# An mLSTM layer on one core: per-chunk rows spread over the partitions by DMA instead of TensorE, and each chunk's heads handled in two halves

## The chip, the cores and the metric

One NeuronCore of a Trainium2 chip runs the whole program. The metric is the device time of one execution in microseconds. Engines are TensorE (PE), VectorE (DVE), ScalarE (ACT), GpSimd (POOL) and SyncE (SP, here only a DMA queue); each executes its own instruction list in order and they meet through semaphores.

## The reference, cut to what matters

With DEPTH = 1 the reference is one layer: an mLSTM mixer and a SwiGLU feed-forward, each behind an RMS norm and with a residual. Sizes: 2048 tokens, width 1024, 8 heads with 64 query/key and 128 value columns, feed-forward width 2816, all float32.

```
u = rmsnorm(x);  q, k, v, o_pre, if_pre = split(u @ w_in)
cum_f = cumsum(log_sigmoid(f));  log_d[t, s] = cum_f[t] - cum_f[s] + i[s]   (s <= t, else -inf)
m_t = max(cum_f + m_state, max_s log_d);  w_inter = exp(cum_f + m_state - m_t)
scores = (q k^T) * exp(log_d - m_t)
num = w_inter * (q C) + scores v;  den = w_inter * (q n) + sum(scores)
h = num / max(|den|, exp(-m_t));  C, n, m carried to the next chunk
x = x + (rms(h) * g * sigmoid(o_pre)) @ w_out;  x = x + swiglu(rmsnorm(x))
```

## The kernel before, in words

The 2048 tokens are worked in two halves of 1024 (`h`). Each half goes through the same stages in turn: norm and transposes of the input (a prologue), the input projection (84 units of 12 matmuls of 128x512, `project`), a chunk loop over 8 chunks of 128 tokens, the second norm, and the feed-forward (`feed_group`, `drain`). Every float32 product is made as three matmuls of a high and a low part (`three_passes`, `project`); the high part is a cast on ACT, the low part a subtraction on DVE. All orders are written out by hand, engine by engine.

The change is in the chunk loop and what feeds it. Gate values (forget sums, their running maximum, the input gate) are computed as rows: tiles `t0` to `t4` of 8 heads x 512 tokens, by `gate_part` on DVE and ACT, spread over the units of the projection by the list `GATE_DVE`. A chunk needs two of these rows on all partitions: minus the running maximum (for the decay matrix) and `w_inter` (for the queries, and its last column for the decay of the state). The kernel before does this on TensorE. `gate_part` stores the rows as high and low parts in `negm` and `wint`, and for each chunk:

- `spread(c)` writes a mask of -1e30 above the diagonal into two PSUM banks by two bf16 matmuls of 128x512 (line 2055) and adds the row of each head by eight matmuls of 128x128 with a selecting matrix `pick` (line 2058). ACT's `decay_matrix` then takes the exponential of each head out of PSUM, with a bias per partition (line 1028).
- `weights(c)` spreads `w_inter` by four matmuls (line 2084), and transposes the keys (line 2090). DVE's `weigh_queries` copies the last column (`dec`, line 1566) and multiplies the queries (line 1569).

The rest of a chunk: `scores` (line 2072), `weigh_keys` (line 1575) and `weigh_scores` (line 1584) on DVE, `state_sums` (line 2139) and `outputs` (lines 2153, 2157) on TensorE. Then DVE's `update_state` (line 1603), ACT's copies into `num` (lines 1085, 1088) and squares, DVE's `head_scale_a` and `head_scale_b`, which end in `hrow` (line 1642). TensorE transposes the eight heads (`turn_heads`, line 2164), DVE gates them (`gate_heads`, line 1591), ACT and DVE split the result (`hg_high`, line 1102; `hg_low`, line 1596), and `out_tile` multiplies with `w_out` (lines 1884 to 1886). DVE adds the product to the residual (`add_out`, line 1651) and in the first chunks prepares `w_out` (`split_out`, line 1528).

TensorE's order in the loop for chunk `c` is: spread, scores, weights(c), the first half of out_tile(c-3, 1), turn_heads(c-1), its second half, state_sums(c), outputs(c), turn_v(c+1), out_tile(c-1, 0). DVE's order is: weigh_queries, weigh_keys, weigh_scores(c), gate_heads(c-1), add_out(c-3, 1), hg_low(c-1), update_state(c), head_scale(c), norm2_rows(c-3), add_out(c-1, 0), and in chunks 1 and 2 a run of split_out. SP issues the loads of a chunk (`load_qkc`, `load_vtc`, `load_og`, 512 KB each) in a fixed order, each behind waits for the buffer it fills. POOL stores the projection and loads the residual tiles (`load_res`, 1 MB each).

Of the kernel before, what the change touches and what calls it, by code (L numbers as in the profile page):

```python
# [5 lines left out]
F32 = mybir.dt.float32  # L6
# [6 lines left out]
P = 128  # L13
# [44 lines left out]
GATE_DVE = (0, 0, 8, 9, 10, 11, 12, 13, 14, 18)  # L58
# [66 lines left out]
def mlstm_layer(nc, x, mix_norm_g, ffn_norm_g, w_gate, w_up, w_down, w_in, b_if, norm_g, w_out, out):  # L125
# [8 lines left out]
    with ExitStack() as ctx:  # L134
# [49 lines left out]
        negm = place("negm", r_a, [P, TOK], F32R)  # L184
        wint = place("wint", r_a + 4 * KB, [P, TOK], F32R)
# [8 lines left out]
        v1 = [place(f"v1_{s}", r_q + 16 * KB + s * HEADS * VW * 4, [P, HEADS, VW], F32) for s in range(2)]  # L194
        dmat = place("dmat", r_c + 12 * KB, [P, HEADS, P], F32)
# [36 lines left out]
        ident_b = small("ident_b", [P, P], BF16)  # L232
        pick = small("pick", [P, HEADS, P], F32R)
        mask = small("mask", [P, 4, P], BF16)
# [7 lines left out]
        dec = small("dec", [P, 4])  # L242
# [6 lines left out]
        pick_src = place("pick_src", r_q, [P, HEADS, P], F32)  # L249
# [10 lines left out]
        h_hbm = nc.dram_tensor("h_hbm", [SEQ // P, P, D], F32, kind="Internal").ap()  # L260
        proj_hbm = nc.dram_tensor("proj_hbm", [HALVES, 3, TILES, P, 8, P], F32, kind="Internal").ap()
# [4 lines left out]
        EPS_SET, IDENT_SET, PICK_SET, CONST_SET = 1, 3, 6, 12  # L266
# [5 lines left out]
        raw_loaded = [sem(f"raw_loaded{s}") for s in range(2)]  # L272
        qkc_loaded = [sem(f"qkc_loaded{s}") for s in range(2)]
# [15 lines left out]
        const_dve = sem("const_dve")  # L289
# [37 lines left out]
        wint_spread = sem("wint_spread")  # L327
# [3 lines left out]
        dec_done = sem("dec_done")  # L331
# [138 lines left out]
        def spread_bank(c):  # L470

            return 0 if c < 2 else 4

# [20 lines left out]
        def _(sp):  # L494
# [25 lines left out]
            for h in range(HALVES):  # L520
                if h == 0:
# [45 lines left out]

                sp.wait_ge(p_lo_done, h * PU + unit_at(10, 6) + 1)
# [16 lines left out]
                load_qkc(2)  # L585
                load_og(1)
# [74 lines left out]
        def _(pool):  # L661
# [6 lines left out]
            nc.gpsimd.memset(pick_src[:, :, :], 0.0).then_inc(const_pool, 1)  # L668
            for row in (0, 32):
                pool.wait_ge(const_pool, 4 + (1 if row else 0))  # L670
                nc.gpsimd.affine_select(out=pick_src[:, :, :], in_=pick_src[:, :, :], compare_op=ALU.not_equal,
                                        fill=1.0, base=-row, pattern=[[-1, HEADS], [0, P]], channel_multiplier=1)\
                    .then_inc(const_pool, 1)
            nc.gpsimd.memset(mask[:, :, :], 0.0).then_inc(const_pool, 1)
# [3 lines left out]
            pool.wait_ge(const_pool, 10)  # L678

            nc.gpsimd.affine_select(out=mask[:, :, :], in_=mask[:, :, :], compare_op=ALU.is_ge, fill=MASKED, base=0,  # L680
                                    pattern=[[0, 4], [1, P]], channel_multiplier=-1).then_inc(const_pool, 1)
# [19 lines left out]
            for h in range(HALVES):  # L701
# [22 lines left out]
                for tile in (cols[:, :], negm[:, :].bitcast(F32), wint[:, :].bitcast(F32)):  # L724
                    nc.gpsimd.memset(tile, 0.0).then_inc(prep_done, 1)

                def store_block(g, k):
# [6 lines left out]
                        .then_inc(p_last_stored if (g, k) == (PG - 1, 1) else p_stored[g % 2], 16)  # L734

# [89 lines left out]
        def _(act):  # L825
# [42 lines left out]
            for h in range(HALVES):  # L868
# [99 lines left out]
                if h == 0:  # L968
                    proj_hi(h, 4)
# [1371 lines left out]
```

## Time and profile before

| | us |
|---|---|
| time, median of 3 runs (lowest, highest) | 2154.73 (2153.97, 2157.39) |
| the profiled execution's own time | 2154.42 |
| its span in the trace | 2152.8 |
| TensorE busy in the span | 2121.9 |
| VectorE busy | 1425.7 |
| ScalarE busy | 939.2 |
| GpSimd busy | 250.1 |

The span is from the first to the last instruction in the trace; the execution's own time has 1.6 us around it. Busy is the time in which an engine had at least one instruction under way. Matmuls overlap in the trace (a 128x512 matmul shows 0.39 us, and one starts every 0.23 us), so what a matmul takes from its successors is read from the distance of starts. The granted clock of TensorE was full over nearly all of the span.

### The profile page before, as it was taken

Reading aid. Unit: us, or ns where it says so; the run is one execution under the profiler, and the core shown is the slowest. Engines: PE = TensorE matmul, PEld = TensorE weight load, DVE = VectorE, ACT = ScalarE, POOL = GpSimd, SP = SyncE. Lnnn points to the kernel's source line nnn. Section 1 sums busy time; section 2 is a strip of 40 time slices with the busy share of each in tenths; the row PEclk is TensorE's granted clock in tenths of the full one; section 3 lists DMA queues with packets and bytes.
Section 4 is the critical chain, followed back from the end, with each engine's and each line's share of the span. In section 5 each row is a group of like instructions: output and inputs, shape, how many; then the busy total and the mean of one; then the engine's idle time right before and its main releaser. Section 6 shows DMA issues by size and latency. Waiting matters only on the chain.

```text
span 2152.8 us, 29471 instructions
## 1 busy us (share of the span) xinstructions
PE 2121.9 (99%) x10424; PEld 1762.6 (82%) x10440; DVE 1425.7 (66%) x2274; ACT 939.2 (44%) x1686; POOL 250.1 (12%) x357
## 2 busy tenths in 40 slices
PE   6999999999999999999999999999999999999999
PEld 5888888888888888888878888888888888888887
DVE  8765476787566565679677644767866657556764
ACT  5433674453333333345444347544533333334443
POOL 3211100021001010100121111001110101001000
PEclk9999999999999999999999999999999999999999
DMA  4333373223322334773414334632233232357443
GB/s 148 110 110 113 109 272 121 84 69 106 105 96 97 117 102 150 270 249 118 152 64 142 118 94 147 233 119 89 68 103 109 97 117 96 105 190 250 152 134 107
DMA packets 200288, 281.56 MB, mean 131 GB/s; under 512 B 12912, under 2 KB 131696, under 8 KB 200176
## 3 DMA queue, kind: packets, MB, share of 16 engines
q1 hardware_dynamic: 171696, 183.07, 26.5%
q0 software_dynamic: 28480, 97.02, 12.9%
q8 instruction: 68, 1.11, 0.2%
q14 instruction: 44, 0.36, 0.1%
HBM read 197.73 MB, written 82.31 MB: 130 GB/s over the span
## 4 chain that ended last, share of the span: by engine, by line
PE 94%; DVE 3%; DMA 1%; ACT 1%; issue 1%; POOL 0%; SPq 0%; DVEq 0%; POOLq 0%
PE ps L2247 13%; PE ps L2250 13%; PE ps L2249 13%; PE ps L1971 7%; PE ps L1975 7%; PE ps L1973 7%; PE ps L2295 6%; PE ps L2297 6%; PE ps L2299 6%; PE ps L1884 3%; PE ps L1886 3%; PE ps L1885 3%; PE ps L1891 2%; PE ps L2157 1%; DMA res<-in_x_dram 1%
## 5 line engine op out<-in xcount | busy, mean ns | idle before, releaser
L1722 DVE TENSOR_TENSOR ring<-raw_f,ring 128x512 fp32r<-128x512 f32 x308 | 211.4, 687 | 188.1 <-ACT ring L1148 186.6
L1148 ACT CAST ring<-raw_f 128x512 fp32r<-128x512 f32 x308 | 191.2, 623 | 208.7 <-PE ps L2250 193.2
L2247 PE MATMUL ps<-u_lo,ring 128*128 128x512 f32 x704 | 275.7, 392 | 0.0
L2250 PE MATMUL ps<-u_hi,ring 128*128 128x512 f32 x704 | 274.1, 389 | 0.0
L2249 PE MATMUL ps<-u_hi,ring 128*128 128x512 f32 x704 | 273.9, 389 | 0.0
L2295 PE MATMUL ps<-ring,ring 128*128 128x512 f32 x616 | 240.5, 390 | 2.0 <-DVE ring L1801 1.9
L2299 PE MATMUL ps<-ring,ring 128*128 128x512 f32 x616 | 239.7, 389 | 0.0
L2297 PE MATMUL ps<-ring,ring 128*128 128x512 f32 x616 | 239.7, 389 | 0.0
L2247 PE MATMUL ps<-t_op,ring 128*128 128x512 f32 x528 | 206.0, 390 | 0.0
L2250 PE MATMUL ps<-t_op,ring 128*128 128x512 f32 x528 | 205.5, 389 | 0.0
L2249 PE MATMUL ps<-t_op,ring 128*128 128x512 f32 x528 | 205.4, 389 | 0.0
L1190 ACT CAST ring<-g_in 128x512 fp32r<-128x512 f32 x154 | 95.6, 621 | 217.4 <-PE ps L2299 215.8
L1795 DVE TENSOR_TENSOR ring<-g_in,ring 128x512 fp32r<-128x512 f32 x154 | 106.3, 690 | 106.0 <-ACT ring L1190 106.0
L795 POOL DMA_DIRECT2D ops_hbm<-kept x154 | 83.6, 543 | 759.1 <-DVE kept L1820 559.6
L1321 DVE TENSOR_TENSOR pring<-raw,pring 128x512 fp32r<-128x512 f32 x132 | 90.7, 691 | 109.7 <-ACT pring L864 108.9
L1815 DVE TENSOR_TENSOR kept<-ps,kept 128x512 f32<-128x512 f32 x132 | 90.9, 689 | 105.7 <-PE ps L2250 105.7
L2250 PEld LDWEIGHTS ps<-u_hi,ring 128*128 128x128 f32 x704 | 132.1, 188 | 27.6
L2247 PEld LDWEIGHTS ps<-u_lo,ring 128*128 128x128 f32 x704 | 132.2, 188 | 27.1 <-issue 0.5
L2249 PEld LDWEIGHTS ps<-u_hi,ring 128*128 128x128 f32 x704 | 132.2, 188 | 26.9
L1971 PE MATMUL ps<-u_lo,pring 128*128 128x512 f32 x384 | 151.7, 395 | 2.4 <-DVE u_lo L1309 2.4
L1975 PE MATMUL ps<-u_hi,pring 128*128 128x512 f32 x384 | 150.3, 391 | 0.0
L1973 PE MATMUL ps<-u_hi,pring 128*128 128x512 f32 x384 | 150.3, 391 | 0.0
(223 smaller groups left out, 4180.3 us busy)
## 6 DMA issues: line engine op xcount, KB each, us to landing
ops_hbm<-kept POOLq DMA_DIRECT2D x154, 256.0 KB, 2.4
g_in<-ops_hbm SPq DMA_DIRECT2D x154, 256.0 KB, 2.7
raw<-in_ml_w_in_dram SPq DMA_DIRECT2D x24, 1024.0 KB, 5.4
proj_hbm<-pkept POOLq DMA_DIRECT2D x96, 256.0 KB, 2.7
raw_f<-in_ffn_w_gate_dram SPq DMA_DIRECT2D x44, 512.0 KB, 4.7
raw_f<-in_ffn_w_up_dram SPq DMA_DIRECT2D x44, 512.0 KB, 4.6
b<-in_ffn_w_down_dram SPq DMA_DIRECT2D x88, 256.0 KB, 4.6
x_in<-in_x_dram SPq DMA_DIRECT2D x16, 512.0 KB, 6.3
```

The lines of the kernel that those rows point to most:

```text
L1148: nc.scalar.copy(four(ring[slot][:, 0, :]), feed_source(q, s)).then_inc(w_hi_done, 1)
L1722: nc.vector.tensor_tensor(four(ring[slot][:, 1, :]), feed_source(q, s), four(ring[slot][:, 0, :].bitcast(F32)), ALU.subtract).then_inc(w_l ...
L1795: nc.vector.tensor_tensor(ring[e % 3][:, 1, :], g_in[e % 4][:, :], ring[e % 3][:, 0, :].bitcast(F32), ALU.subtract).then_inc(ea_lo_done, 1)
L1971: pe.matmul(banks(bank), w[:, 0, now], moved(kind, 1, k), start=(fresh and k == 0), stop=False, skip_group_check=True)
L1973: pe.matmul(banks(bank), w[:, 0, now], moved(kind, 0, k), start=False, stop=False, skip_group_check=True)
L1975: last = pe.matmul(banks(bank), w[:, 1, now], moved(kind, 0, k), start=False, stop=(k == 3), skip_group_check=True)
L2247: pe.matmul(banks(bank), wh, moved(kind, 1, k), start=(fresh and k == 0), stop=False, skip_group_check=True)
L2249: pe.matmul(banks(bank), wh, moved(kind, 0, k), start=False, stop=False, skip_group_check=True)
L2250: last = pe.matmul(banks(bank), wl, moved(kind, 0, k), start=False, stop=(k == 3), skip_group_check=True)
L2295: pe.matmul(banks(bank + j), a[:, 0, now], w[:, 1, :], start=(fresh and n == 0), stop=False, skip_group_check=True)
L2297: pe.matmul(banks(bank + j), a[:, 0, now], w[:, 0, :], start=False, stop=False, skip_group_check=True)
L2299: last = pe.matmul(banks(bank + j), a[:, 1, now], w[:, 0, :], start=False, stop=(n == GROUPS - 1), skip_group_check=True)
```

## The change

The rows go out to a DRAM tensor and come back spread over the partitions.

- `negm`, `wint`, `pick`, `ident_b`, `dec`, TensorE's `spread` and the first half of `weights` go (what is left is `turn_keys`), and so do step 9 of `gate_part` and two ACT copies per call of it.
- POOL's `store_rows` writes `t4` and `t2` of each half of the gate rows to `rows_hbm`, after projection groups 1 and 4. SP's `load_rows(c)` reads them back: one DMA for `negb` (8 heads x 128 tokens, the same for 128 partitions, 512 KB) and two for `wq` (one head of each pair for each half of the partitions, 256 KB together). It stands ahead of the first load of `w_out` for chunks 0 and 1, and right behind `load_qkc(c)` from chunk 2 on, with waits for the slot's readers.
- DVE's `mask_rows(c)` adds the mask to `negb` in place. It stands within the last projection group for chunks 0 and 1, and between hg_low(c-1) and update_state(c) for chunk c+1.
- `weigh_queries` and `update_state` read `wq`; `decay_matrix` reads `negb`, from SBUF.
- `hrow` is made, transposed and gated in two halves of four heads. `h_done` and `h_turned` now count halves.
- `load_res(0)` moves ahead of the last projection store. A few steps of the prologue, of the second norm and of the passage to the second half change places. TensorE's unit 83 is now cut in two equal parts around `turn_keys(1)` and `turn_v(1)`.

```diff
+                def store_rows(t):
+                    for kind, tile in ((0, t4), (1, t2)):
...
+                        pool.dma_start(rows_hbm[h, kind, 4 * t:4 * t + 4, :].rearrange("c (p n) -> p c n", n=P),
+                                       tile[:, :].rearrange("p (c n) -> p c n", n=P)).then_inc(rows_stored, 16)
+                def load_rows(c):
+                    s = c % 2
+                    if c >= 2:
+                        sp.wait_ge(dmat_done, h * 64 + 8 * (c - 1))
+                        sp.wait_ge(qw_done, h * 8 + c - 1)
+                        sp.wait_ge(state_done, h * 32 + 4 * (c - 1))
+                    sp.dma_start(negb[s][:, :, :].rearrange("p i t -> p (i t)"),
+                                 rows_hbm[h, 0, c:c + 1, :].partition_broadcast(P)).then_inc(negb_loaded[s], 16)
+                    for a in range(2):
+                        rows = rows_hbm[h, 1, c, :].rearrange("(g a n) -> a g n", a=2, n=P)
+                        sp.dma_start(wq[s][64 * a:64 * a + 64, :, :], rows[a].partition_broadcast(64))\
+                            .then_inc(wq_loaded[s], 16)
                 load_qkc(2)
+                load_rows(2)
                 load_og(1)
...
                 for c in range(3, TILES):
                     load_qkc(c)
+                    load_rows(c)
                     load_vtc(c)
+                def mask_rows(c):
+                    dve.wait_ge(negb_loaded[c % 2], h * 64 + 16 * (c // 2) + 16)
+                    nc.vector.tensor_tensor(negb[c % 2][:, :, :], negb[c % 2][:, :, :],
+                                            mask[:, :].unsqueeze(1).broadcast_to([P, HEADS, P]), ALU.add)\
+                        .then_inc(darg_done, 1)
                     if c:
                         hg_low(c - 1)
+                        if c + 1 < TILES:
+                            mask_rows(c + 1)
                     update_state(c)
-                def spread(c):
-                    for half in range(2):
-                        pe.matmul(banks(spread_bank(c) + half), ident_b[:, :], mask[...], start=True, stop=False)
-                        for i in range(4):
-                            last = pe.matmul(ps[...], pick[:, 4 * half + i, :], negm[:, now], stop=(i == 3))
-                    for g in range(4):
-                        last = pe.matmul(ps[:, 2, g * P:g * P + P], pair, wint[:, tile_cols(c)], ...)
 def gate_heads(c):
+                    for half in range(2):
+                        some = slice(4 * half, 4 * half + 4)
+                        dve.wait_ge(h_turned, h * 16 + 2 * c + half + 1)
+                        last = nc.vector.tensor_tensor(og[c % 2][:, some, :], ..., og[c % 2][:, some, :], ALU.mult)
 def turn_heads(c):
+                    for half in range(2):
+                        pe.wait_ge(h_done, h * 16 + 2 * c + half + 1)
+                        for i in range(4 * half, 4 * half + 4):
+                            last = pe.transpose(ps[:, 4 + half, ...], hrow[:, i, :], ident[:, :])
+                        last.then_inc(h_turned, 1)
 the second norm
-                feed_low(0, 3)
                 op_lo(st + 1, 5)
+                feed_low(0, 3)
```

## Rows read from the trace of the kernel before

**Rows 1.** The page, parts 1 and 4: busy time; the chain that ended last, by engine.
```profile
PE 2121.9 (99%) x10424; PEld 1762.6 (82%) x10440; DVE 1425.7 (66%) x2274; ACT 939.2 (44%) x1686; POOL 250.1 (12%) x357
...
PE 94%; DVE 3%; DMA 1%; ACT 1%; issue 1%; POOL 0%; SPq 0%; DVEq 0%; POOLq 0%
```
**Rows 2.** TensorE's instructions by line: busy us, mean ns, idle before.
```profile
L2058 PE MATMUL ps<-negm,pick 128*128 128x128 f32 x128 | 22.0, 309 | 0.0
L2084 PE MATMUL ps<-wint,pick 128*128 128x128 f32 x64 | 10.3, 283 | 0.0
L2055 PE MATMUL ps<-mask,ident_b 128*128 128x512 bf16 x16 | 6.2, 390 | 0.0
```
**Rows 3.** Windows (us of the span): busy PE, PEld, DVE, ACT, POOL; clock, DMA share, GB/s.
```profile
264.00:330.00 66.00, 63.91 (x470) 54.12 (x472) 46.17 (x91) 42.38 (x86) 6.18 (x11) 1.00 0.65 239
330.00:411.00 81.00, 81.00 (x581) 68.90 (x584) 52.48 (x112) 33.77 (x76) 2.92 (x5) 1.00 0.35 118
```
**Rows 4.** Timeline, a steady chunk: start, duration, engine, line, what [idle before].
```profile
340.45 0.10 PEld L2055 LDWEIGHTS ps<-mask,ident_b 128*128 128x128 bf16 x1 [0.26 <-issue]
...
341.80 1.16 PE L2072 MATMUL ps<-qkc 64*128 64x128 f32 x16
...
342.89 0.66 PE L2084 MATMUL ps<-wint,pick 128*128 128x128 f32 x4
...
343.39 0.63 PE L2090 MATMUL ps<-ident,qkc 128*128 128x128 f32 x4
...
344.40 0.68 DVE L1575 TENSOR_TENSOR kw<-ps,colt 128x512 f32<-128x512 f32 x1
...
350.34 1.10 PE L2139 MATMUL ps<-v,kw 128*64 128x129 f32 x16
...
351.12 1.22 DVE L1596 TENSOR_TENSOR hg_lo<-og,hg_hi 128x1024 fp32r<-128x1024 f32 x1
...
354.56 1.13 DVE L1603 SCALAR_TENSOR_TENSOR state<-state,dec,ps 128x129 f32<-128x129 f32 x4 [2.21 <-PE ps L2157]
```
**Rows 5.** Timeline, chunk 0 into chunk 1 of the first half.
```profile
283.20 1.41 DVE L1528 SCALAR_TENSOR_TENSOR wo<-wo_raw,head_g,wo 128x512 fp32r<-128x512 f32 x2 [1.61 <-ACT wo L1010]
...
284.59 1.13 DVE L1603 SCALAR_TENSOR_TENSOR state<-state,dec,ps 128x129 f32<-128x129 f32 x4
...
292.43 1.06 PE L2164 MATMUL ps<-ident,hrow 128*128 128x128 f32 x8 [0.99 <-DVE pkept L1456]
```
**Rows 6.** Timeline, chunk 1 into chunk 3 of the first half.
```profile
296.30 1.23 DVE L1596 TENSOR_TENSOR hg_lo<-og,hg_hi 128x1024 fp32r<-128x1024 f32 x1 [1.11 <-ACT hg_hi L1102]
...
297.64 1.13 DVE L1603 SCALAR_TENSOR_TENSOR state<-state,dec,ps 128x129 f32<-128x129 f32 x4
...
305.36 0.69 DVE L1651 TENSOR_TENSOR res<-ps,res 128x512 f32<-128x512 f32 x1 [0.68 <-DMA res<-in_x_dram]
...
309.45 1.10 PE L2139 MATMUL ps<-v,kw 128*64 128x129 f32 x16 [0.86 <-DVE kw L1575]
...
322.03 2.73 DVE L1528 SCALAR_TENSOR_TENSOR wo<-wo_raw,head_g,wo 128x512 fp32r<-128x512 f32 x4
...
330.07 1.10 PE L2139 MATMUL ps<-v,kw 128*64 128x129 f32 x16
```
**Rows 7.** Timeline, the same place of chunk 2 in the second half.
```profile
1368.85 0.69 DVE L1651 TENSOR_TENSOR res<-ps,res 128x512 f32<-128x512 f32 x1 [1.56 <-DMA res<-in_x_dram]
...
1372.94 1.10 PE L2139 MATMUL ps<-v,kw 128*64 128x129 f32 x16 [1.74 <-DVE kw L1575]
```
**Rows 8.** Timeline, the second norm of the first half.
```profile
453.39 1.22 DVE L1309 TENSOR_TENSOR u_lo<-ps,u_hi 128x1024 fp32r<-128x1024 f32 x1
...
454.66 1.09 PE L1891 MATMUL ps<-ident,res 128*128 128x128 f32 x8 [0.89 <-DVE u_lo L1309]
```
**Rows 9.** DMA issued near 289.2 us: queue, size, us to landing.
```profile
og<-proj_hbm SPq DMA_DIRECT2D x1, 512.0 KB, 6.5
```
**Rows 10.** The same for the DMA issued at 297.6 us.
```profile
og<-proj_hbm SPq DMA_DIRECT2D x1, 512.0 KB, 12.5
```
**Rows 11.** DMA issued between 330 and 411 us, steady chunks.
```profile
og<-proj_hbm SPq DMA_DIRECT2D x4, 512.0 KB, 4.4
```
**Rows 12.** Timeline, the prologue of the first half.
```profile
47.03 0.93 PE L1891 MATMUL ps<-ident,t_rows 128*128 128x128 f32 x4 [1.26 <-DVE t_op L1309]
```

More of the change, by code:

```diff
@@ L194, in mlstm_layer @@
         v1 = [place(f"v1_{s}", r_q + 16 * KB + s * HEADS * VW * 4, [P, HEADS, VW], F32) for s in range(2)]
+        wq = [place(f"wq{s}", r_a + (4 + 2 * s) * KB, [P, 4, P], F32) for s in range(2)]
         dmat = place("dmat", r_c + 12 * KB, [P, HEADS, P], F32)
@@ L231, in mlstm_layer @@
         ident = small("ident", [P, P])
-        ident_b = small("ident_b", [P, P], BF16)
-        pick = small("pick", [P, HEADS, P], F32R)
-        mask = small("mask", [P, 4, P], BF16)
+        mask = small("mask", [P, P])
+        negb = [place("negb0", r_a, [P, HEADS, P], F32), small("negb1", [P, HEADS, P])]
         not_first = small("not_first", [HEADS, NB], BF16)
@@ L666, in _ @@
                                     pattern=[[-1, P]], channel_multiplier=1).then_inc(const_pool, 1)
[L668 to L674, printed above, removed]
+            nc.gpsimd.memset(mask[:, :], 0.0).then_inc(const_pool, 1)
             nc.gpsimd.memset(not_first[:, :], 1.0).then_inc(const_pool, 1)
@@ L888, in gate_part @@
                             .then_inc(gate_act, 1)
-                        nc.scalar.copy(negm[0:HEADS, now], t4[:, :]).then_inc(gate_act, 1)
                     if step == 2:
@@ L1547, in _ @@
                     for t in range(2):
-                        for step in range(2, 10):
+                        for step in range(2, 9):
                             if n == GATE_DVE[step] + GATE_NEXT * t:
                                 gate_part(t, step)
+                    if n == unit_at(PG - 1, 0):
+                        mask_rows(0)
+                    if n == unit_at(PG - 1, 2):
+                        mask_rows(1)
                     if n == unit_at(PG - 1, 3):
@@ L2045, in _ @@
                 turn_unit(st, 15)
[L2046 to L2060 removed]
+                pe.wait_ge(gate_dve, 2 * h * 12 + 5)
                 def scores(c):
@@ L2081, in weights @@
                         pe.wait_ge(num_kept, h * 16 + 2)
-                    for g in range(4):
-                        pair = pick[:, :, :].rearrange("p h c -> p (h c)")[:, 2 * g * P + DQK:2 * g * P + DQK + P]
-                        last = pe.matmul(ps[:, 2, g * P:g * P + P], pair, wint[:, tile_cols(c)],
-                                         start=(g == 0), stop=(g == 3), skip_group_check=True)
-                    last.then_inc(wint_spread, 1)
                     if c < 2:
@@ L2161, in turn_heads @@
                 def turn_heads(c):
-                    pe.wait_ge(h_done, h * 8 + c + 1)
-                    for i in range(HEADS):
-                        last = pe.transpose(ps[:, 4 + i // 4, (i % 4) * P:(i % 4) * P + P], hrow[:, i, :],
-                                            ident[:, :])
-                    last.then_inc(h_turned, 1)
+                    for half in range(2):
+                        pe.wait_ge(h_done, h * 16 + 2 * c + half + 1)
+                        for i in range(4 * half, 4 * half + 4):
+                            last = pe.transpose(ps[:, 4 + half, (i % 4) * P:(i % 4) * P + P], hrow[:, i, :],
+                                                ident[:, :])
+                        last.then_inc(h_turned, 1)
                 def out_tile(c, jj, k0, k1):
@@ L2184, in _ @@
                 outputs(0)
-                spread(1)
-                project(PU - 1, 0, 1)
-                weights(1)
+                project(PU - 1, 0, 2)
+                turn_keys(1)
                 turn_v(1)
-                project(PU - 1, 1, 4)
+                project(PU - 1, 2, 4)
                 scores(1)
```

155 lines of the change are left out of this document (68 added, 87 removed).

## Prediction

> **What bounds the kernel now.** I read the page first, then TensorE's groups by line, then windows by stage, then the timeline of the chunk loops, and the DMAs by time of issue. The page says that TensorE is busy 2121.9 of 2152.8 us and makes 94% of the chain that ended last [rows 1]. So the question is which removed matmuls stood in line, and where something else comes up when they go. The windows split the chunk loop in two. Chunks 3 to 7 (330 to 411 us) have TensorE busy for all of 81 us, with DVE at 52.5 and ACT at 33.8 [rows 3]; they are bound by TensorE alone. Chunks 0 to 2 (264 to 330) have 2.1 us of TensorE idle, which shows that DVE is about to end last there [rows 3], and its waits sit in front of turn_heads(0) and state_sums(2) [rows 5, 6]. The second half repeats both. In the first part removing TensorE work can't be expected to pay; in the second it should pay in full.
>
> **What goes on TensorE.** By busy time the three groups are 22.0 + 10.3 + 6.2 = 38.5 us [rows 2], but a matmul's record overlaps the next, and half of the bf16 records are missing (16 of 32), so I go by starts. In a steady chunk spread begins at 340.45 and scores at 341.80: 1.35 us. w_inter's four matmuls run from 342.89 to the start of the key transposes at 343.39: 0.50 us [rows 4]. Together 1.85 us per chunk, 29.6 us over 16 chunks.
>
> **Steady chunks (c = 4 to 7, both halves).** One chunk takes 350.34 - 330.07 = 20.27 us from state_sums to state_sums [rows 4, 6], and would take 18.4. What DVE gets: mask_rows, a 128x1024 addition with both inputs in SBUF, for which I take hg_low's 1.22 us (same shape, both inputs in SBUF) [rows 4]; dec's copy (under 0.2 us) goes; and two pairs of half instructions. A 128x512 one costs 0.68 to 0.69 us (2.73 for four) against 1.22 for 1024 columns [rows 4, 6], so each pair costs 0.14 more. DVE was busy 52.5 of 81 us, 13.1 per chunk; it becomes 13.1 + 1.22 + 0.28 - 0.15 = 14.5 of 18.4, and has room. The order matters too: mask_rows follows hg_low, which ends at 352.34, and update_state starts at 354.56 after an idle 2.21 us [rows 4]. It fits there and costs nothing; without that cover it would cost up to 1.22. The chain to the next state_sums has slack: kw is done at 345.08 and used at 350.34 [rows 4], 5.3 us, and after the change 5.3 - 1.85 = 3.4, less 0.3 for the halves. decay_matrix no longer waits for spread; ACT has room. An ACT exponential out of SBUF instead of PSUM isn't in the trace; between half its time and half as much again it stays under that slack, and I take no difference. So 8 chunks save 1.85 each: **14.8 us**.
>
> **Chunks 0 to 3 (their 1.85 us each are mostly lost).** I follow DVE.
> Chunk 0: TensorE gets to its outputs up to 1.85 us earlier, but update_state(0) at 284.59 stands behind split_out, which ends at 284.61 [rows 5] and is set by ACT, whose row of copies, exponentials and splits starts from turn_v(0), which doesn't move. ACT wins only the 0.2 us it waited for spread. turn_keys(1) waits for that update. TensorE reaches turn_heads(0), now at 292.43 after a wait for the last add_unit [rows 5], about 0.15 us earlier; 0.14 goes to the halved hrow.
> Chunk 1: hg_low(0) ends at 297.53 and update_state(1) starts at 297.64 [rows 6]; no gap as in the steady chunks. mask_rows(2) goes between, so the update is about 1.1 us later, and with it the copies, squares, h_done(1) and DVE's list behind. Against that add_out(0, 0) no longer waits 0.68 us for load_res(0), which is issued some 10 us sooner [rows 6], and 0.1 us of dec goes. The waits for state_sums(2) end at 309.45 now [rows 6], and at 309.8 to 309.9 after.
> Chunk 2: the same again with mask_rows(3); h_done(2) is about 2 us later, then add_out and four split_out, which end at 324.76 now [rows 6] and near 326.9 after. The second half of out_tile(0, 1) needs the last of them: TensorE waits about 1 us there, runs 2.7 us, and is at state_sums(3) near 329.95, against 330.07 [rows 6]. Net 0.1 us.
> Second half: there add_out(0, 0) waited 1.56 us for its DMA and state_sums(2) 1.74 for kw [rows 7], 0.88 more in each case, which the earlier load_res gives back. Net 1.0 us. **Together 1.1 us** of the 14.8 that the matmuls of chunks 0 to 3 were worth; the bounds are a loss of 3 (both masks wholly late, in both halves) and all 14.8.
>
> **The DMAs.** 768 KB more per chunk, 12 MB in all. In steady chunks a 512 KB load lands after 4.4 us [rows 11]; load_rows(c+1) can issue about 6 us into chunk c-1, when its update is done, and mask_rows wants it about 15 us later. load_vtc behind it comes 1 to 1.5 us later and has over 10 us. Free. The tight one is load_rows(2): issued near 289.1, wanted at 297.5. Its neighbour landed after 6.5 us [rows 9], while one issued at 297.6 needed 12.5 [rows 10]. Three issues in place of one and 1 MB of residual ahead put it at 296 to 298; I take no wait. load_vtc(3) behind load_rows(3) may cost TensorE up to 1 us per half.
> The Trainium skill, DMA: Bandwidth & Descriptors, section Issuing engines are not separate DMA queues, says that transfers from the sync and GpSimd engines run on the same 16 DMA engines and interleave. The 12.5 us of [rows 10], with POOL's 1 MB residual loads in flight, agree. By it the residual load that I moved ahead delays the rows; were the queues separate, the rows would land after about 4.4 us and never be waited for. It supports the DMA rival below.
>
> **Second norm.** op_lo(5) goes ahead of feed_low(0, 3), a 0.68 us instruction; the transposes at 454.66 waited 0.89 us for it [rows 8]. 0.6 us per half, **1.2 us**.
>
> **Prologue and passage.** Constants for `pick` go, hidden before x arrives. With op_hi(0, 3) ahead of norm1_sum(4) DVE waits about 1.2 us for proj_hi(1), which op_lo(4) ahead of proj_lo(3) mostly gives back. op_lo(7) ahead of proj_sums takes the 1.26 us wait at 47.03 [rows 12], but project(4) behind it still needs op_lo(8) at the same time. I take 0, between a loss of 2 and a gain of 2. The gate rows' copies, POOL's stores and the waits on them lie beside a TensorE that is busy throughout; 0.
>
> **Sum.** 14.8 + 1.1 + 1.2 = 17.1 us off the profiled execution's own 2154.42: **2137.3 us**, 0.8% less. The median of the runs shown is 2154.73, 0.3 above that execution, well within the spread.
>
> **Rivals.**
> 1. Every removed start counts, because DVE's early chain finds room (the ordering of halves lets TensorE and DVE overlap, chunk 1 has ACT waits to close). 29.6 + 1.2 = 30.8 us off: 2123.6. For it speaks how little TensorE idles (2.1 us in 66) [rows 3]; against it that the idle it has is all behind DVE and that the gap before update_state(1) is 0.1 us [rows 6].
> 2. The rows land late in the crowded stretch. If load_rows(2) takes the 12.5 us of [rows 10], it is there at 302, 4.5 us after DVE wants it, and DVE, which stands with everything behind mask_rows, passes it on to state_sums(2): 9 us in two halves. 2137.3 + 9 = 2146.
> 3. Slower. load_rows stands in every chunk between load_qkc and load_vtc on one in-order queue, and mask_rows stands before update_state. If the row spread from one 4 KB source came so slowly that it landed over 15 + 3 + 1.85 = 20 us after issue, every steady chunk would be longer than its 20.27. At 24 us, twice the worst 512 KB load seen [rows 10], 4 us for 12 chunks: 48 us less the 17 gives 2185. Against it: 4.4 us in steady chunks at a DMA share of 0.35 [rows 3, 11].
> 4. The change does nothing: the gain sits in cover and TensorE simply waits for DVE, 2154. The full 81 us of TensorE in 81 us speak against it [rows 3].
>
> **Chances and range.** The forecast 0.67, rival 1 0.12, rival 2 0.13, rival 3 0.03, rival 4 0.05. Within the forecast the early chunks and the prologue may each move it by some 4 us: 2131 to 2142. The range reaches towards both neighbours, 2127 to 2146. 0.2% is 4.3 us, about what a measurement can tell here. Faster: the forecast, rivals 1 and 2 (2146 is 0.4% less), and a little off for worse mixtures, 0.92. Same 0.04, slower 0.04.
>
> **What would show each step.** TensorE's lines 2055, 2058 and the first four of 2084 are gone, and steady chunks last 18.4 us with TensorE at 99 to 100%. DVE's mask addition shows 1.2 us, with no wait on a DMA in front of it (a wait there is rival 2), and between hg_low(0) and update_state(1) it pushes. TensorE's idle in the chunks 0 to 3 grows from 2.1 to 8 or 9 us in each half, behind kw, state and wo. The wait before add_out(0, 0) for the residual is gone. The forecast is wrong if steady chunks last more than 19 us or the first three get shorter by more than 3.

## The result, and the profile after

The changed kernel takes 2143.31 us (median of 5 runs, 2140.89 to 2145.86), the kernel before 2154.73 in the same job (2153.97 to 2157.85). The ratio is 0.9938, 95% interval 0.9927 to 0.9949 (the two medians alone give 0.9947): faster by 0.5 to 0.6%. The prediction was 2137.3 with 2127 to 2146 as its range: the sign and the range hold, and a third of the forecast gain of 17.1 us is missing. Its profiled execution took 2145.86 with a span of 2144.2, the slowest of the five; spans below are compared with the 2152.8 of the kernel before.

The page of the kernel after, parts 1 and 4. TensorE has lost 21.5 us of busy time against [rows 1], and a DMA (vtc) has come into the chain that ended last, whose DMA share went from 1% to 3%:
```profile
PE 2100.4 (98%) x10216; PEld 1740.8 (81%) x10216; DVE 1435.3 (67%) x2296; ACT 937.0 (44%) x1678; POOL 246.1 (11%) x358
...
PE 92%; DMA 3%; DVE 2%; ACT 2%; issue 1%; SPq 0%; POOL 0%; DVEq 0%; ACTq 0%; POOLq 0%
```
The two windows of [rows 3] after the change (length, busy PE, PEld, DVE, ACT, POOL, clock, DMA share, GB/s). In the steady chunks TensorE is still busy for all of 81 us; in chunks 0 to 2 it idles 9.6 us, and the DMA share is 0.79 in place of 0.65:
```profile
264.00:330.00 66.00, 56.44 (x406) 46.98 (x405) 49.70 (x96) 41.02 (x83) 5.59 (x10) 0.95 0.79 273
330.00:411.00 81.00, 81.00 (x590) 68.03 (x589) 60.43 (x128) 37.92 (x82) 3.43 (x6) 1.00 0.47 153
```
A steady chunk after, to be read beside [rows 4]: start, duration, engine, line, what [idle before]. State_sums follows 18.52 us behind the one before it (331.84), and mask_rows lies between hg_low and update_state, which still waits 1.08 us for TensorE:
```profile
346.66 1.04 PE L2167 MATMUL ps<-ident,hrow 128*128 128x128 f32 x8
...
350.36 1.10 PE L2140 MATMUL ps<-v,kw 128*64 128x129 f32 x16
...
351.14 1.22 DVE L1618 TENSOR_TENSOR hg_lo<-og,hg_hi 128x1024 fp32r<-128x1024 f32 x1
...
352.27 1.22 DVE L1544 TENSOR_TENSOR negb<-negb,mask 128x1024 f32<-128x1024 f32 x1
...
354.57 1.13 DVE L1625 SCALAR_TENSOR_TENSOR state<-state,wq,ps 128x129 f32<-128x129 f32 x4 [1.08 <-PE ps L2159]
```
Chunk 1 into chunk 3 of the first half, which answers to [rows 6]. In front of the mask addition stands a wait of 1.60 us for its rows; update_state(1) starts at 299.22 in place of 297.64; state_sums(2) waits 3.22 us for kw and its matmuls then take 1.99 us in place of 1.10; turn_v(3) waits for vtc:
```profile
295.25 1.23 DVE L1618 TENSOR_TENSOR hg_lo<-og,hg_hi 128x1024 fp32r<-128x1024 f32 x1 [1.11 <-ACT hg_hi L1119]
...
298.07 1.22 DVE L1544 TENSOR_TENSOR negb<-negb,mask 128x1024 f32<-128x1024 f32 x1 [1.60 <-DMA negb<-rows_hbm]
...
299.22 1.12 DVE L1625 SCALAR_TENSOR_TENSOR state<-state,wq,ps 128x129 f32<-128x129 f32 x4
...
310.26 1.99 PE L2140 MATMUL ps<-v,kw 128*64 128x129 f32 x16 [3.22 <-DVE kw L1593]
...
317.28 1.09 PE L2108 MATMUL ps<-ident,vtc 128*128 128x128 f32 x8 [0.88 <-DMA vtc<-proj_hbm]
...
331.84 1.10 PE L2140 MATMUL ps<-v,kw 128*64 128x129 f32 x16
```
The window 300 to 306 us shows the DMA engines full (share 1.05, 403 GB/s), with the clock still whole, and one of the second half a clock of 0.77:
```profile
300.00:306.00 6.00, 4.63 (x34) 3.56 (x33) 4.26 (x15) 4.56 (x9) 0.71 (x1) 1.00 1.05 403
...
1366.00:1372.00 6.00, 4.14 (x38) 3.73 (x39) 4.74 (x8) 2.78 (x8) 0.00 (x0) 0.77 1.03 337
```
The transfers behind these waits, by time of issue (near 287.5, 301.8 and 303.5; the number is us to landing), and last the negb loads of steady chunks, issued between 340 and 400:
```profile
negb<-rows_hbm SPq DMA_DIRECT2D x1, 512.0 KB, 10.5
...
negb<-rows_hbm SPq DMA_DIRECT2D x1, 512.0 KB, 13.4
...
vtc<-proj_hbm SPq DMA_DIRECT2D x1, 512.0 KB, 13.7
...
negb<-rows_hbm SPq DMA_DIRECT2D x2, 512.0 KB, 4.3
```

**Where the time went.** Read the start of state_sums(0), (3) and (7) in both halves, from the two traces. The forecast's split comes from its own terms.

| stretch | before | after | gained | forecast |
|---|---|---|---|---|
| up to state_sums(0), first half | 280.37 | 277.61 | 2.76 | 1.85 |
| state_sums(0) to (3), first half | 49.70 | 54.23 | -4.53 | -1.73 |
| (3) to (7), first half | 81.00 | 74.06 | 6.94 | 7.4 |
| to state_sums(0), second half | 931.92 | 929.03 | 2.89 | 2.45 |
| (0) to (3), second half | 50.59 | 57.02 | -6.43 | -0.85 |
| (3) to (7), second half | 81.00 | 74.07 | 6.93 | 7.4 |
| to the end | 678.22 | 678.18 | 0.04 | 0.6 |

The gains add to 8.60 us, the difference of the spans (11.4 by medians; the profiled execution of the changed kernel is the longest of its five). Of the 8.5 that are missing here from 17.1, 8.4 lie in state_sums(0) to (3): 2.80 in the first half and 5.58 in the second. The experiments are about these two stretches. I call their length, by the starts of state_sums, L; the forecast had it at 51.4 in both halves.

One trace is one execution. The first row contains a difference of TensorE's clock in the prologue, and L moves by some us between kernels that should agree (experiment 5), so a small difference in L is read only where the waits or the clock of the two traces explain it.

### The profile page after: what moved, and what is told of

It reads as the page before. It is cut to its first block, busy times and chain, and to the rows that moved or that the text cites. A ratio compares the mean times of both kernels' runs of the same rounds, so it can differ in the third digit from the quotient of the medians.

```text
span 2144.2 us, 29137 instructions
## 1 busy us (share of the span) xinstructions
PE 2100.4 (98%) x10216; PEld 1740.8 (81%) x10216; DVE 1435.3 (67%) x2296; ACT 937.0 (44%) x1678; POOL 246.1 (11%) x358
## 3 DMA queue, kind: packets, MB, share of 16 engines
q8 instruction: 66, 1.08, 0.2%
## 4 chain that ended last, share of the span: by engine, by line
PE 92%; DMA 3%; DVE 2%; ACT 2%; issue 1%; SPq 0%; POOL 0%; DVEq 0%; ACTq 0%; POOLq 0%
PE ps L2251 13%; PE ps L2250 13%; PE ps L2248 13%; PE ps L1997 7%; PE ps L2001 7%; PE ps L1999 7%; PE ps L2296 6%; PE ps L2300 6%; PE ps L2298 6%; PE ps L1910 3%; PE ps L1912 3%; PE ps L1911 3%; PE ps L1917 2%; DMA vtc<-proj_hbm 1%; PE ps L2159 1%
```

## Experiments

Theory A: the rows add 768 KB a chunk to a stretch in which the 16 DMA engines are already full in part (share 1.04 from 300 to 306 us in the kernel before), so rows and vtc land late. Rivals: B, the mask's 1.2 us in DVE's gapless chain; C, the halves; D, the clock, which fell to half behind TensorE's new gaps. Each time is a median beside runs of the kernel before on the same chip (2155.15, 2155.66 and 2155.42 in the three jobs), each ratio is to those. The ratios are estimated from all runs and differ from the quotient of the medians by up to 0.1%.

**1. No row loads from chunk 2 on.**
```
 def load_rows(c):
     if c >= 2:
+        return
 ...                     # the waits for negb and wq then count only the first two loads
```


> The changed kernel, but the row loads (negb, wq) are issued for chunks 0 and 1 only; chunks 2 to 7 use those rows again (it leaves out reading the rows of chunks 2 to 7, so 9 MB less is moved). Theory A (the rows' DMAs are what chunks 0 to 3 lost: vector engine waits 1.6 us for negb at 298.07, 1.6 and 0.7 in the second half; TensorE waits 0.9 and 2.0 us for vtc behind them, and the clock is halved for 6.8 and 10.2 us after the gaps): 4 to 6 us less than the changed kernel, near 2138, no wait on negb and under 0.5 us on vtc in chunks 0 to 3, state_sums(3) near 329.8. Theory B (the loss is the mask addition of 1.2 us in the gapless chain of the vector engine): the waits on DMAs go but TensorE meets the same waits for kw and state a little earlier, at most 2 us less. Theory C (the halved instructions and the exponential out of SBUF): no difference, within 1 us.

2137.86 us, ratio 0.9922 (0.9908 to 0.9935). L is 51.29 and 51.20, the forecast's 51.4. TensorE's waits for vtc and DVE's for negb are gone, that for kw in front of state_sums(2) stays (3.1 us where the changed kernel has 3.2). The trace:
```profile
264.00:330.00 66.00, 60.02 (x431) 50.12 (x429) 51.03 (x98) 42.19 (x85) 5.57 (x10) 0.95 0.67 237
```
TensorE idles 6.0 us in place of 9.6, at the same clock of 0.95. Theory A holds. The time is also the forecast's for the case that no row is late, though not term by term (see below).

**2. Which rows: only those of chunks 2 and 3 left out.**
```
+    if c in (2, 3):
+        return
```


> The changed kernel without the row loads of chunks 2 and 3 alone (these two chunks use the rows of chunks 0 and 1; it leaves out reading their own); those of 4 to 7 are loaded. Theory A, sharper (only the loads that fall into the saturated stretch of chunks 0 to 2 cost): all of what the kernel without row loads from chunk 2 on gained, near 2138, ratio to the kernel before 0.992. Rival (row loads cost in every chunk, by queue time or shared engines): a third of it for two chunks of six, near 2141.5.

2136.90 us, ratio 0.9911 (0.9896 to 0.9926); L 50.55 and 52.30. Two chunks of six bring all of it. In chunks 4 to 7 the rows are free, as predicted.

The two halves of this trace, with no wait for a DMA in either, show what the clock costs. Behind state_sums(2) it is whole in the first half and mostly at the lower level in the second:
```profile
308.00:315.00 7.00, 4.66 (x54) 4.35 (x55) 5.89 (x9) 2.85 (x7) 0.00 (x0) 1.00 0.37 146
1364.00:1371.00 7.00, 6.88 (x49) 6.34 (x50) 5.33 (x6) 2.28 (x3) 0.00 (x0) 0.56 0.11 20
```
State_sums(2) to (3) takes 19.56 us in the first and 21.32 in the second, 1.8 more. So the clock can lengthen L by itself, and rival D isn't nothing.

**3. The mask on one head of eight.**
```
-    negb[:, :, :] + mask            (8 heads)
+    negb[:, 0:1, :] + mask, c >= 2  (1 head)
```


> The changed kernel, with the mask added to one head of eight from chunk 2 on (it leaves out most of the causal mask there), so the addition costs some 0.2 us instead of 1.22. Theory A (late rows): the vector engine waits for the rows all the same, so update_state(1) moves only from 299.22 to about 298.2; 1 to 2 us less in all. Theory B (the mask's 1.2 us in the gapless chain of chunks 1 and 2, twice in each half): up to 2 x 2 = 4 us less, near 2139, from state_sums(2) and state_sums(3) 1 and 2 us earlier. Both: nothing in steady chunks, 18.52 us each.

2146.05 us, ratio 0.9956 (0.9942 to 0.9970): nothing gained. L is 55.28 and 54.56. With a lighter DVE chain (its waits for negb fall from 3.9 to 2.9 us) TensorE meets vtc instead, 4.8 us in two places against 2.9 in the changed kernel. The two lists of waits, TensorE's rows for vtc, first of the changed kernel, then of this one (total, times, longest):
```profile
PE ps L2108 <- DMA vtc<-proj_hbm: 2.9, 2, 2.0
```
```profile
PE ps L2109 <- DMA vtc<-proj_hbm: 4.8, 2, 4.1
```
B as the sole cause falls; it could still count once the DMAs are in time (experiment 9).

**4. Filler to hold the clock.**
```
+    7 matmuls 128x512 ahead of turn_keys(1)
+    12 matmuls 128x128 behind scores(1)
+    12 matmuls 128x512 ahead of state_sums(2)
```


> The changed kernel, with extra matmuls whose results nobody reads, in the places of chunks 0 to 2 where TensorE stands idle (7 of 128x512 ahead of the key transposes of chunk 1, 12 small ones behind scores(1), 12 of 128x512 ahead of state_sums(2)). Theory D (the idle gaps make the granted clock fall to half, 6.8 us in the first half and three stretches of 3.4 us in the second, and the work in these stretches takes twice as long): the clock stays at 1.00, state_sums(3) comes 2 to 3 us earlier in each half, 3 to 5 us less in all, near 2139. Against it: where the vector engine sets the end of the chunk, TensorE's slower work hides beside it and the clock costs nothing; then the same time or, where the filler itself pushes, 1 to 3 us more.

2146.82 us, ratio 0.9964 (0.9950 to 0.9978); L 56.19 and 55.08. The granted clock, changed kernel first, then with filler:
```profile
308.00:314.00 6.00, 3.74 (x32) 3.41 (x32) 5.10 (x8) 1.84 (x5) 0.00 (x0) 0.50 1.06 351
```
```profile
308.00:314.00 6.00, 5.50 (x52) 4.48 (x51) 5.47 (x8) 1.86 (x6) 0.00 (x0) 1.00 1.06 335
...
318.00:321.00 3.00, 3.00 (x12) 2.69 (x11) 1.97 (x6) 2.44 (x3) 0.71 (x1) 0.52 1.05 384
```
State_sums(2) and outputs(2) ran at 2.4 GHz, and TensorE then stood 2.72 us at turn_v(3), which began at 317.62 against 317.28 without filler:
```profile
317.62 1.97 PE L2108 MATMUL ps<-ident,vtc 128*128 128x128 f32 x8 [2.72 <-DMA vtc<-proj_hbm]
```
So in the first half the slow stretch in front of turn_v(3) cost nothing: TensorE waits for vtc(3) until 317.3 to 317.6 with it and without it. The filler only moved the half clock behind the new wait. It also stands in TensorE's way: state_sums(0) to (1) takes 15.52 us in both halves, against 14.70 without it, so this run isn't a clean test of the clock.

Behind turn_v(3) the clock does cost. From there to state_sums(3) TensorE takes 14.49 to 14.56 us in every trace in which the clock had fallen in front of turn_v(3) alone, as in the changed kernel's first half (14.56). It takes 15.98 to 16.21 where the clock falls behind it: both halves of this run and of experiment 10, the second halves of experiment 3 and of the changed kernel (16.21, clock 0.51):
```profile
1375.74 1.69 PE L2108 MATMUL ps<-ident,vtc 128*128 128x128 f32 x8 [2.03 <-DMA vtc<-proj_hbm]
...
1376.00:1379.00 3.00, 3.00 (x13) 2.61 (x12) 1.96 (x6) 2.43 (x3) 0.71 (x1) 0.51 0.87 310
```
The difference of the changed kernel's two halves is 1.7 us. In all of these cases the fall follows TensorE's wait for the late vtc. Experiment 1 has the same 0.95 over the window and the full gain; there the clock is low from 285 to 289 and from 310 to 312, in front of turn_v(3).

**5. Whole heads again.**
```
-    for some in (slice(0, 4), slice(4, 8)): hrow ... .then_inc(h_done, 1)
+    hrow (8 heads) ... .then_inc(h_done, 2)   # turn_heads, gate_heads likewise
```


> The changed kernel with each chunk's heads scaled, turned and gated whole again, as before the change. Prediction's step: each pair of half instructions costs the vector engine 0.14 us more, 0.3 per chunk, and TensorE's transposes may start 0.6 us earlier. In steady chunks both hide: 18.52 us either way. In chunks 0 to 2 the halves let the chain run 0.5 us shorter per chunk if the vector engine sets the pace, so whole heads would be 1 to 2 us slower than the changed kernel, near 2145. Rival (DMA sets the pace there): no difference, within 1 us of 2143.3.

2144.23 us, ratio 0.9945 (0.9931 to 0.9958), not to be told from the changed kernel. L is 54.31 in the first half, where turn_v(3) starts at 317.39, and 53.27 in the second, where the changed kernel's trace has 57.02. This trace is of the fastest of its five executions (2142.23) and the changed kernel's of the slowest (2145.86); the medians differ by 0.9 us the other way, so the 3.75 us aren't credited to the whole heads. In steady chunks the period is 18.52 either way. The halves are worth nothing measurable here. C falls.

**6. Other bulk moved out.**
```
 load_vtc(1)
+gain row (512 KB)              # was between the two halves of wo
-residual 1, 2, 3 in chunks 1, 2, 3
+residual 1, 2, 3 in chunks 2, 4, 5
```


> The changed kernel with all its work, but 1.5 MB of other loads moved out of the saturated stretch: the gain row (512 KB) is issued behind load_vtc(1), near 273.5, where the DMA share is 0.2, and the residual quarters 1 to 3 are issued in chunks 2, 4 and 5 in place of 1, 2 and 3. Theory A (what is short is DMA throughput at about 400 GB/s; 1.5 MB are 3.7 us of it): no waits on rows, vtc waits under 0.5 us, clock as it may be, 4 to 6 us less than the changed kernel, near 2138.5. Rival (it is the form of the row loads, 128 partitions from one 4 KB source, or their place in the queue, not the total of bytes): rows land as late as before the move, at most 1.5 us less.

2140.79 us, ratio 0.9934 (0.9921 to 0.9948): the median is 2.5 us under the changed kernel's, but the intervals overlap. L is 51.29 and 52.49; the waits for vtc are gone, those for negb went from 3.9 us in three places to 1.5 in one. The timed gain is smaller than in the trace, so this run alone wouldn't carry theory A. The gain row also leaves the sync engine's queue here, so the run doesn't part the bytes from the place in that queue; experiment 10 does.

**7. The same, and vtc ahead of the rows.**
```
 load_qkc(c)
-load_rows(c)
 load_vtc(c)
+load_rows(c)
```


> The kernel with the bulk moved, and from chunk 3 on load_vtc ahead of load_rows in the queue. load_vtc(3) waits only for TensorE's turn of v(2) and load_rows(3) for update_state(1), so vtc is issued later than the rows could be. Theory A: vtc(3) is what TensorE waits for (0.9 and 2.0 us) while the rows of chunk 3 have slack; ahead of 768 KB of rows it lands about 1.9 us sooner: 0 to 2 us less than the kernel with the bulk moved alone. Rival: the rows come late in place of vtc (the vector engine waits for negb), 0 to 2 us more.

2139.55 us, ratio 0.9921 (0.9907 to 0.9934), L 52.25 and 51.16. Against experiment 6 it is 1.2 us less, inside the spread. One wait for negb, 1.1 us, was left.

**8. The same, and negb(2) issued early.**
```
 gain row
+load_negb(2)      # waits for the exponentials of chunk 0 alone
 ...
-load_rows(2)
+load_wq(2)
```


> The kernel with the bulk moved and vtc first, in which the decay rows of chunk 2 (negb, 512 KB) are issued right behind the gain row, near 279, as soon as the exponentials of chunk 0 have read that buffer, in place of near 288.5; wq(2) stays. The kernel it starts from still had the vector engine wait 1.1 us for negb at 299.5 in one half. Theory A (the late rows are what is left of the DMA cost): no wait on negb, up to 1 us less than 2139.5. Rival (what is left is the vector engine's own chain with the mask addition): within 1 us of it.

2136.64 us, ratio 0.9919 (0.9906 to 0.9933). The issue came at 276.56, 11 us sooner than the 287.52 of the changed kernel, and no wait for negb or vtc is left. L is 51.15 and 50.52, at or a little under the forecast's length, with all row loads in place. The two halves run the same orders, with the same 3.15 to 3.19 us of wait in front of state_sums(2); what parts them is the clock behind it, and 20.21 us against 19.58 to state_sums(3):
```profile
310.00:313.00 3.00, 3.00 (x23) 2.77 (x20) 1.89 (x4) 1.64 (x3) 0.00 (x0) 0.50 0.04 11
1364.00:1367.00 3.00, 3.00 (x33) 2.88 (x34) 1.89 (x4) 1.33 (x2) 0.00 (x0) 1.00 0.15 51
```
The early issue was tried only with the bulk moved as well; what it is worth alone isn't shown.

**9. The same, and the mask in DVE's gap.**
```
 gate_heads(c - 1)
+mask_rows(c + 1)
 hg_low(c - 1)
-mask_rows(c + 1)
```


> The same, and mask_rows(c+1) stands behind gate_heads(c-1) in place of behind hg_low(c-1). Between these two the vector engine waits 1.11 us while the scalar engine makes hg_hi, and the addition takes 1.22. Theory (once no DMA is late, the mask's 1.2 us in the gapless chain of chunks 1 and 2 set the pace, as the prediction had it: about 1 us late in chunk 1 and 2 us in chunk 2): 1 us less for each of these chunks, 2 to 4 us in two halves, near 2136. Rival (TensorE's own work of the chunk sets its length now): no more than 1 us. In steady chunks 18.52 us either way.

2135.41 us, ratio 0.9909 (0.9894 to 0.9924). The mask runs while ACT makes hg_hi, and hg_low follows without the 1.11 us of idle time seen above at 295.25:
```profile
292.89 1.28 DVE L1621 TENSOR_TENSOR og<-ps,og 128x512 f32<-128x512 f32 x2
294.09 1.21 DVE L1554 TENSOR_TENSOR negb<-negb,mask 128x1024 f32<-128x1024 f32 x1
...
295.28 1.23 DVE L1628 TENSOR_TENSOR hg_lo<-og,hg_hi 128x1024 fp32r<-128x1024 f32 x1
296.56 1.12 DVE L1635 SCALAR_TENSOR_TENSOR state<-state,wq,ps 128x129 f32<-128x129 f32 x4
```
L is 50.02 and 50.51: 1.1 us less than in experiment 8 in the first half, although a wait of 0.4 us for negb came back there. In the second half L is the same: state_sums(0) to (1) took 0.65 us longer, with the clock at 0.50 from 1345 to 1348, and (1) to (3) 0.66 less. The median is 1.2 us less than in 8, inside the spread. So B is real but small: the 1.0 us of chunk 1 shows in the first half (state_sums(1) to (2), 16.24 to 15.25), where 2 to 4 were expected in all. This is the fastest version, 20.0 us under the kernel before, and its interval lies clear of the changed kernel's.

**10. The first residual quarter back in its place.**
```
-load_res(0) at the last projection unit
+load_res(0) behind the copies of chunk 0
```


> The changed kernel with the first residual quarter (1 MB) issued again behind the copies of chunk 0, near 290, as in the kernel before, in place of 285.4. Prediction's step: the vector engine then waits for it before add_out(0, 0), 0.7 to 1.6 us in each half. Theory A (throughput is short): with the rows of chunk 2 ahead of the megabyte they land in time (no wait of 1.6 us on negb), and the residual lands late: the two about cancel, within 1.5 us of 2143.3. Rival (order in time doesn't matter to the rows): the waits for the residual come on top, 2 to 3 us slower than the changed kernel.

2144.18 us, ratio 0.9948 (0.9935 to 0.9962), the same as the changed kernel within the spread. DVE's waits for negb fell from 3.9 to 0.7 us, and 0.6 for the residual came in two places. Negb(2), the same load at the same place of its own queue (issued at 289.15), landed after 6.0 us in place of 10.5 (10.5 in experiments 3 and 5 too); what had gone from ahead of it is POOL's megabyte:
```profile
negb<-rows_hbm SPq DMA_DIRECT2D x1, 512.0 KB, 6.0
```
So neither the form of the row loads nor their place in the sync engine's queue is enough to make them late. But TensorE waited 6.8 us for vtc in place of 2.9; L is 54.95 and 55.40. The issue came at 296.14 in place of 285.39, later than the 290 I expected, since a store stood ahead of it on POOL. In a full stretch a megabyte moved by 10 us changes who waits, and the sum stays.

**11. The orders alone, in the kernel before.**
```
 op_hi(0, 3) ahead of norm1_sum(0, 4); op_lo(4), op_lo(7), op_lo(8), op_lo(st + 1, 5)
 each ahead of the norm, sum, projection or feed_low that it stood behind; passage likewise
```


> The kernel before, with only the changed orders: op_hi(0, 3) and op_lo ahead of the norms, sums and projections of the prologue, op_lo(5) ahead of feed_low in the second norm, and the passage. The prediction gave 1.2 us for the second norm and nothing for the prologue. The changed kernel shows 1.1 us in the prologue and nothing in the second norm. Theory (orders are worth what the traces show): 1 to 2 us less than the kernel before, near 2153. Rival (the orders pay only with the lighter rest, or cost something): within 0.5 us of the kernel before.

2155.01 us, ratio 1.0001 (0.9992 to 1.0010): nothing. Where the gate's projection starts in the prologue, kernel before, orders alone, changed kernel:
```profile
59.05 0.50 PE L1989 MATMUL ps<-u_lo,if_w 128*128 128x512 f32 x1 [0.54 <-DVE u_lo L1309]
```
```profile
59.66 0.50 PE L1987 MATMUL ps<-u_lo,if_w 128*128 128x512 f32 x1 [0.54 <-DVE u_lo L1307]
```
```profile
58.01 0.50 PE L2015 MATMUL ps<-u_lo,if_w 128*128 128x512 f32 x1 [0.54 <-DVE u_lo L1326]
```
The changed kernel's 1.0 us there isn't the orders' doing alone: most of it is TensorE's clock. The kernels of experiments 2, 3, 7 and 10 have the changed kernel's prologue, and start this matmul at 59.55 to 59.88; the changed kernel and the others with it start it at 57.94 to 58.05. The first group has a clock of 0.91 from 40 to 60 us, the second 1.00. Kernel before, changed kernel, experiment 3:
```profile
40.00:60.00 20.00, 17.75 (x95) 14.40 (x95) 18.03 (x21) 9.41 (x12) 5.96 (x4) 0.91 0.00 1
```
```profile
40.00:60.00 20.00, 16.61 (x98) 13.61 (x97) 17.79 (x22) 9.21 (x12) 5.96 (x4) 1.00 0.00 0
```
```profile
40.00:60.00 20.00, 16.56 (x91) 13.73 (x90) 16.42 (x20) 9.05 (x12) 5.96 (x4) 0.91 0.00 0
```
So 1.6 us of the changed kernel's prologue belong to the execution and not to the kernel. The kernel before has this difference too, smaller: 59.05 here at 0.91, 58.44 in experiment 12 at 1.00. Of the 1.0 us between the two traces 0.6 are the clock and 0.4 the orders, and at 0.91 the orders lose 0.6 instead (59.05 and 59.66). The gain of 2.76 up to state_sums(0) contains this.

The orders of the passage to the second half do show a gain. From state_sums(7) of the first half to state_sums(0) of the second takes 931.92 us before, 930.80 with the orders alone and 929.03 in the changed kernel, whose matmuls account for 1.85. TensorE's waits for its operands there, kernel before and orders alone (480 to 1330 us: total, times, longest):
```profile
PE ps L2295 <- DVE ring L1801: 1.9, 2, 1.2
```
```profile
PE ps L2293 <- DVE ring L1799: 0.8, 2, 0.6
```
In the time of a whole execution these 1.1 us are lost among the differences of the prologue and of L.

**12. The bulk moved in the kernel before.**
```
 the edit of experiment 6, in the kernel before
```


> The kernel before, with the same 1.5 MB moved out of the stretch (gain row early, residual quarters 1 to 3 later). Theory A (in the kernel before the stretch had 2.3 MB less and nothing but the first residual quarter came late, 0.7 and 1.6 us): at most 1.5 us less than the kernel before, 2153 to 2155. Rival (the moved loads are worth 2 to 4 us in any kernel, so that what they gained says nothing of the change): 2151 to 2152.

2153.94 us, ratio 0.9994 (0.9985 to 1.0003): within what a measurement can tell. So making room is worth nothing here before the rows have filled it; after, it is worth the 2.5 us of experiment 6, as far as these can be told from the spread.

## Why the prediction was right, and where it was off

**Steady chunks: right.** Forecast 14.8 us, measured 6.94 + 6.93 = 13.9 from state_sums(3) to (7). The period went from 20.25 on average to 18.52, 1.73 in place of 1.85. The mask addition costs 1.22 us (mean 1219 ns over 16), as taken from hg_low, and lies in the gap that was named for it; the halves are 0.68 to 0.69 us each. All three show in the trace and none in the time. DVE went to 60.4 of 81 us; the forecast's 14.5 of 18.4 per chunk is 64.

**Chunks 0 to 3: the step that failed.** "Three issues in place of one and 1 MB of residual ahead put it at 296 to 298; I take no wait." negb(2) was issued at 287.52, 1.6 us sooner than taken, took 10.5 us and landed near 298.0: the date lay at the far end of that span, but DVE now wanted it at 296.5, not at 297.5, because hg_low(0) ended 1.1 us earlier. That is a wait of 1.60. In the second half it was 1.6 for chunk 2 and 0.7 for chunk 3. The bigger part was the second sentence, vtc(3) behind the rows "up to 1 us per half": 0.9 and 2.0 us, and a floor below everything ahead of it, which is why experiments 3 and 4 won nothing. Against experiment 1, L is 2.9 us longer in the first half: 1.4 up to state_sums(2), behind the late negb, and 1.4 to turn_v(3), behind the late vtc. In the second half it is 5.8 longer: 1.7, 2.4, and 1.7 more behind turn_v(3), where the clock fell after the wait. The prediction had no term for the clock. The forecast had rival 2 (rows late in the crowded stretch, 0.13) as a case of its own with 9 us; what came is six tenths of it, 5.4 us by the medians of experiment 1 and of the changed kernel (5.9 when each is counted from its own runs of the kernel before), on top of a forecast that was otherwise met to 0.6 us: 2137.86 without the late rows, 2137.3 forecast. That this sum was met so closely is in part luck: steady chunks brought 0.9 us less and the second norm 1.2 less, the passage brought 1.0 more, and the profiled execution that the forecast started from had the low clock in its prologue. The chip did neither case whole: the time lies between them.

The Trainium skill, DMA: Bandwidth & Descriptors, section Issuing engines are not separate DMA queues, says that transfers issued by different engines run on the same 16 DMA engines, which spoke for that rival. The runs agree with it: moving the one megabyte that POOL issues changed when the sync engine's rows landed (10.5 us in the changed kernel, 6.0 in experiment 10), and so did moving loads of both engines (8.5 in experiment 6).

**The chain in DVE's order: right in kind, too dear.** The prediction had the mask push update_state by 1.1 us in chunk 1 and 2 in chunk 2. Without late rows TensorE idles 6.0 us in the window 264 to 330, where the prediction had 8 or 9 (experiment 1), and taking the mask out of the chain brings 1.1 us in one half (experiment 9): the 1.1 of chunk 1 is there, the second 1.1 of chunk 2 isn't seen. L of 51.2 and 51.3 in experiment 1 is near the forecast's 51.4 although the clock fell in both halves, which costs 0.6 us in experiment 8 and isn't in the forecast. The 9.6 us of idle in the changed kernel are near the forecast by accident, since part of them is DMA.

**The residual: the wait went as forecast, and it was worth nothing.** The wait of 0.68 and 1.56 us before add_out(0, 0) is gone, but the earlier megabyte delays the rows, and putting it back changes nothing (experiment 10): what the rows win, vtc loses.

**The second norm: wrong, 1.2 us.** The wait of 0.89 [rows 8] is gone, and two others stand in the same passage, 0.28 and 0.57, together 0.85; the kernel before with the orders alone shows the same two. TensorE simply meets the next late operand:
```profile
448.89 1.09 PE L1917 MATMUL ps<-ident,res 128*128 128x128 f32 x8 [0.28 <-DVE u_lo L1326]
...
451.95 0.66 PE L1917 MATMUL ps<-ident,t_second 128*128 128x128 f32 x4 [0.57 <-DVE t_op L1326]
```
**Prologue: 0 taken, 0.9 more than the matmuls measured in the trace**, inside its bounds of 2; the larger part is the clock of the two executions, and the orders can as well lose 0.6 there (experiment 11). **Passage: 0 taken, 1.0 measured**, and this one is the orders' doing.

**Rivals 1, 3 and 4** are out: L grew, so not every removed start counted; the rows cost nothing in steady chunks (experiment 2), where negb lands in 4.3 us, far from 20; and the steady chunks took their gain all but 0.9 us of it.

## What to carry to other kernels

Matmuls that build a broadcast are a fair trade for a DMA where TensorE is the bound, and the trade is made stage by stage: price the bytes at the stage's own free rate, and not at the landing time of a quiet stage. When traces of two kernels are set side by side, look at the granted clock of each stretch first: here it moved 1.6 us in a prologue that the change hardly touches. Where the DMA share is near 1, a load's landing doesn't move with the engine that waits for it, so gains ahead of it vanish; look for a quiet window before the stage and split the load so that its part with the fewest waits goes there. In an engine's fixed order, put new work into a gap that the trace shows, not where it reads best.

## What the runs showed of the hardware

A DMA issue on the sync engine takes 0.32 us in quiet times and up to 3.00 in the crowded stretch, and the issue behind it in the queue starts only then. A full share alone doesn't do it: the issues at 301.36 and 301.80 took 0.33 and 0.37 us, and those behind them 1.25 (for two) and 3.00, all at a share of 1.05. From the changed kernel's timeline of that engine:
```profile
273.20 0.32 SPq L563 DMA_DIRECT2D vtc<-proj_hbm  x1
...
287.52 1.20 SPq L553 DMA_DIRECT2D negb<-rows_hbm  x1
288.78 2.02 SPq L557 DMA_DIRECT2D wq<-rows_hbm  x2
...
303.50 3.00 SPq L563 DMA_DIRECT2D vtc<-proj_hbm  x1
```
In the changed kernel the clock stood at 0.50, the lower of its two levels (1.2 of 2.4 GHz), from 308 to 314 us. TensorE had waited 1.37 us at 305.87 and then 3.22 us up to 310.26, and state_sums(2) took 1.99 us in place of 1.10. The wait alone doesn't fix the date: in experiment 8 waits of 3.15 and 3.19 us left state_sums(2) at 1.10 in both halves, with the clock falling behind it in one half and not in the other. What a fall costs depends on what ends last behind it: nothing in front of the late vtc(3) (experiment 4), 0.6 us in experiment 8, 1.8 in experiment 2, and 1.7 behind turn_v(3) in the changed kernel's second half.

An exponential of 128x128 takes ACT 387 ns from SBUF and 384 from PSUM (means over 32 in the steady chunks of the two kernels), so the prediction's choice of no difference was right.
